# Shifting the start addresses of weights, operands and working buffers in SBUF by 32, 96 and 192 bytes

## What is computed

```
first block (1 layer):   x += g1 * ((gated sum of conv, HGRN2 and stick-breaking branches) @ w_out)
                         x += g2 * (square(relu(h2 @ mlp_w1)) @ mlp_w2)
second block (2 layers): x += 0.5 * swiglu(rms(x), ffn1_w_gate, ffn1_w_up, ffn1_w_down)
                         x += (sig(g_attn) * y_attn + sig(g_rnn) * y_rnn) @ w_out
                         x += 0.5 * swiglu(rms(x), ffn2_w_gate, ffn2_w_up, ffn2_w_down)
```

## Time and profile before

| | |
|---|---|
| median of three runs | 3328.55 us |
| profiled execution | 3327.95 us |
| its span, first to last instruction | 3326.2 us |
| granted TensorE clock | 0.999 |
| TensorE matmul busy | 3306.1 us, 17742 matmuls |
| weight loads busy | 2799.9 us |
| VectorE, ScalarE, GpSimd busy | 2169.9, 1466.6, 2127.7 us |

### The profile page before, as it was taken

The page is one execution under the profiler, slowest core; times in us unless marked ns, Lnnn a source line. Parts: engine busy times, 40 slices in busy tenths (PEclk is TensorE's granted clock), DMA queues, the critical chain, the costliest instruction groups (busy, mean ns, idle before and its releaser), DMA issues.

```text
span 3326.2 us, 52762 instructions
## 1 busy us (share of the span) xinstructions
PE 3306.1 (99%) x17742; PEld 2799.9 (84%) x17742; DVE 2169.9 (65%) x3377; ACT 1466.6 (44%) x2025; POOL 2127.7 (64%) x2188
## 2 busy tenths in 40 slices
PE   9999999999999999999999999999999999999999
PEld 5888777888889997788888899889987888888998
DVE  8887685544478878714435877788878334248886
ACT  4365664222243335735634333433347545533333
POOL 6444445555568886653356888698876544468886
PEclk9999999999999999999999999999999999999999
DMA  6221553322232323332223323232223222223232
GB/s 224 88 70 64 168 181 108 104 95 96 97 112 94 107 82 102 102 127 70 70 84 110 108 101 114 76 114 101 101 89 109 95 102 70 83 92 111 102 109 99
DMA packets 94485, 343.36 MB, mean 103 GB/s; under 512 B 10609, under 2 KB 11249, under 8 KB 93954
## 3 DMA queue, kind: packets, MB, share of 16 engines
q1 hardware_dynamic: 86978, 312.11, 27.4%
q10 hardware_dynamic: 7360, 29.29, 2.7%
HBM read 335.03 MB, written 2.13 MB: 101 GB/s over the span
## 4 chain that ended last, share of the span: by engine, by line
PE 52%; POOL 23%; issue 18%; DVE 2%; ACT 2%; DVEq 1%; POOLq 0%; ACTq 0%; DMA 0%
POOL w_lo L588 22%; PE ps L634 15%; PE ps L636 15%; PE ps L635 15%; POOL t_lo L588 1%; PE ps L1217 1%; PE ps L1199 1%; PE ps L801 1%; PE ps L802 1%; PE ps L803 1%; DVE arena L2771 1%; PE ps L1208 0%; DVEq L2773 0%; ACT w_hi L1305 0%; DVE arena L2172 0%
## 5 line engine op out<-in xcount | busy, mean ns | idle before, releaser
L588 POOL TENSOR_TENSOR w_lo<-raw,w_hi 128x256 fp32r<-128x256 f32 (+1 forms) x1680 | 1467.9, 904 | 1051.9 <-ACT w_hi L1305 1049.8
L634 PE MATMUL ps<-a_hi,w_lo 128*128 128x512 f32 (+1 forms) x2720 | 1019.3, 375 | 0.8 <-DVE a_lo L2118 0.3
L636 PE MATMUL ps<-a_hi,w_hi 128*128 128x512 f32 (+1 forms) x2720 | 1005.6, 370 | 0.0
L635 PE MATMUL ps<-a_lo,w_hi 128*128 128x512 f32 (+1 forms) x2720 | 1005.3, 370 | 0.0
L588 POOL TENSOR_TENSOR w_lo<-arena,w_hi 128x512 fp32r<-128x512 f32 x384 | 586.0, 1551 | 124.7 <-ACT w_hi L1785 121.3
L634 PEld LDWEIGHTS ps<-a_hi,w_lo 128*128 128x128 f32 x2720 | 512.6, 188 | 101.0 <-issue 18.3
L1305 ACT ACTIVATE w_hi<-raw 128x1024 fp32r<-128x1024 f32 x374 | 392.6, 1053 | 442.5 <-PE ps L636 424.0
L636 PEld LDWEIGHTS ps<-a_hi,w_hi 128*128 128x128 f32 x2720 | 512.6, 188 | 88.1
L635 PEld LDWEIGHTS ps<-a_lo,w_hi 128*128 128x128 f32 x2720 | 513.0, 189 | 81.2 <-issue 0.5
L634 PE MATMUL ps<-b_hi,w_lo 128*128 128x512 f32 x1088 | 425.9, 391 | 4.8 <-DVE b_lo L2190 4.0
L635 PE MATMUL ps<-b_lo,w_hi 128*128 128x512 f32 x1088 | 424.0, 390 | 0.0
(11 more groups left out here) (332 smaller groups left out, 4706.3 us busy)
## 6 DMA issues: line engine op xcount, KB each, us to landing
raw<-in_stream SPq DMA_DIRECT2D x471, 512.0 KB, 3.3
arena<-in_stream SPq DMA_DIRECT2D x96, 512.0 KB, 3.3
arena<-in_mod_w ACTq DMA_DIRECT2D x32, 512.0 KB, 4.2
arena<-in_mod_w SPq DMA_DIRECT2D x16, 512.0 KB, 11.6
arena<-arena ACTq DMA_DIRECT2D x16, 256.0 KB, 3.7
arena<-cum_rows ACTq DMA_DIRECT2D x2, 2048.0 KB, 9.2
xres<-in_x_t SPq DMA_DIRECT2D x4, 512.0 KB, 5.4
arena<-in_first SPq DMA_DIRECT2D x8, 256.0 KB, 11.8
```

The costliest lines, as they stand in the source:

```text
L588: last = pool.tensor_tensor(to[:, at], of[:, at], hi[:, at].bitcast(F32), ALU.subtract)
L634: pe.matmul(out, lo, x_hi, start=start, stop=False)
L635: pe.matmul(out, hi, x_lo, start=False, stop=False)
L636: return pe.matmul(out, hi, x_hi, start=False, stop=stop)
```

## The change

Three buffers that nothing reads or writes are put between the others, of 32, 64 and 96 bytes a partition:

```
         raw = sb("raw", [P, RING, D])
+        sb("shift_weights", [P, 8])
         w_hi = sb("w_hi", [P, RING, D], F32R)
         w_lo = sb("w_lo", [P, RING, D], F32R)
 
+        sb("shift_operands", [P, 16])
         a_hi, a_lo = sb("a_hi", [P, KT, S], F32R), sb("a_lo", [P, KT, S], F32R)
         b_hi, b_lo = sb("b_hi", [P, KT, S], F32R), sb("b_lo", [P, KT, S], F32R)
+        sb("shift_back", [P, 24])
         xres = sb("xres", [P, KT, S])
```

## The result

The changed kernel takes 3334.11 us (median of 20 runs, 3332.34 to 3334.91) against 3328.57 us (20 runs, 3327.69 to 3329.93): a ratio of 1.0016, interval 1.0009 to 1.0022. It is slower by 5.5 us, less than the 0.2% that the prediction counted as a change, and not the 28 us faster that it forecast.

What follows compares the result with a forecast made beforehand. The prediction took TensorE's matmul pitches as the bound: 28.2 us gained on a, b and streamed w, zero for all else, took 3327.95 to 3299.8 us, median 3300.3 us. The range was 3245 to 3375 us, the forecast's own 3283 to 3318.

Steps and rivals of the forecast that it cites:

- TensorE's pitches are the bound; no instruction moves; loads, rounding and subtraction take the same: Whole kernel: TensorE busy 3306.1 of 3326.2 us; issue cost nil, loads and ScalarE and GpSimd accesses costed at zero.
- What sets `t` and `q11` apart from `a` is where they start: 256-column matmuls: starts 32 bytes past a multiple of 64 give fixed parts of 11.3 and 10.0 ns, against 13.3.
- If the fixed part falls as it did there: 12,480 x 2.26 = 28.2 us: Matmuls on a, b and streamed w: each pitch's part beyond its columns shrinks 2.26 ns, gaining 28.2 us.
- The sign that the prediction named for 256 columns on `a`: Timeline after, 256 columns on a: pitch of some 117.7 ns where 120.0 stood.
- the one for 512 columns: Timeline after, undisturbed projection with 512 columns: pitch about 224.5 ns, against 226.8 before.
- `t` and `q11`: zero taken, between -4 and +6 us for `t`: Matmuls on t and q11, remainder by 64 now equal to the weights': zero; q11 between 0 and plus 2.5 us.
- At 1% other engines hold back little; GpSimd isn't the bound at 251 of 300 us: Fast chunks: GpSimd, busy 251.33 of 300 us, still isn't the bound with TensorE 1% quicker or itself 1% slower.
- No even step: Rival, 512-column stream: pitch stays at about 231.3 ns, 45 us slower, 3374 us; chance 0.22.
- Distance alone: Rival: only stream distance modulo 64 counts; t and q11 fall back to 120.0 ns, 8.7 us, 3337 us; chance 0.06.
- Nothing changes: Rival: a and b keep their distance from the weights modulo 64, t doesn't react; 3328.6 us; chance 0.17.

Runs made afterwards that it cites:

- common_shift32: Kernel before with weights, a, b, t, q11 and the working buffers all 32 bytes further, distances unchanged; 3328.83 us, ratio 1.0001.
- w32_only: Kernel before with only the rounded weights moved, to remainder 32 by 128; 3380.93 us, ratio 1.0157.
- back64_only: Kernel before with only t, q11 and the working buffers moved, to remainder 64 by 128; 3330.26 us, ratio 1.0005.

## Why the prediction was wrong

- *TensorE's pitches are the bound; no instruction moves; loads, rounding and subtraction take the same.* Right in the main. Loads into `raw` and the arena still land in 3.3 us, rounding takes 1061 ns as in the earlier trace rows (grouped view of the changed kernel below), GpSimd's subtraction of 512 columns takes 1361 ns from `raw` and 1562 from the arena in the mean, 1359 and 1551 before, and the pitches sum to the span's change. (These means differ by the buffer in either kernel; the two single rows, 1.30 and 1.31 us, didn't show it.)

```profile
L1788 ACT ACTIVATE w_hi<-arena 128x1024 fp32r<-128x1024 f32 x192 | 203.8, 1061 | 412.4 <-PE ps L639 412.4
```

- *What sets `t` and `q11` apart from `a` is where they start.* Wrong, and the root of the rest. In the earlier trace rows the moving start and its distance from the weights differ together; the prediction saw both and took the first. common_shift32 separates them: `a` at 32 with the weights at 32 keeps 120.0 ns with 256 columns and 226.7 with 512.

- *If the fixed part falls as it did there: 12,480 x 2.26 = 28.2 us.* **The step that failed**, carried from 256 to 512 columns because one pair of pitches (120.0 and 226.8) had the same fixed part. Measured: +17.2 us on the 9,984 with 512 columns; on the 960 short ones that stream `w` -5.0 us, more than twice the 2.2 us that the term gives them. On `a` itself, at the same new starts, the fixed part rose with 512 columns from 13.3 to 228.9 - 213.4 = 15.5 ns and fell with 256 to 117.8 - 106.7 = 11.1 ns. The sign that the prediction named for 256 columns on `a`, some 117.7 ns for 120.0, came; the one for 512 columns, 224.5 ns, came out the other way.

- *`t` and `q11`: zero taken, between -4 and +6 us for `t`.* The size was off and the bound too tight: without the waits `t` went from 364.3 to 353.4 us, 10.9 less. In the runs `t` stood anywhere from 113.3 to 120.2 ns, and the earlier trace rows showed one of these values.

- *At 1% other engines hold back little; GpSimd isn't the bound at 251 of 300 us.* Wrong where it mattered. The stretch view after still has GpSimd at 253.48 of 300 us:

```profile
2205.00:2505.00 300.00, 299.38 (x1965) 272.29 (x1964) 242.15 (x344) 114.65 (x137) 253.48 (x193) 1.00 0.28 97
```

But `t` got 4% faster, not 1%, and that mean hides the 15 us of each chunk in which GpSimd works without a gap (the rows above); 7.1 us more than before were waited at their end, (6.2 + 2.4) - (1.2 + 0.3). Part 4 of the page of the kernel before, the chain of work that ended last, had a sign of it that the prediction didn't use, GpSimd with 23%:

```profile
PE 52%; POOL 23%; issue 18%; DVE 2%; ACT 2%; DVEq 1%; POOLq 0%; ACTq 0%; DMA 0%
```

- *The rivals.* "No even step" had the mechanism, with 2.2 ns per long matmul instead of 4.5. It allowed the short ones 2,496 x 2.26 = 5.6 us; with `t` and `q11` they gave back 12.6, and the rest is 5.5 us, under the 0.2% counted as a change. w32_only shows what lay one shift away: 233.3 ns and 3381 us, above the range. "Distance alone" came nearest in time (3337 us for 3334.1), by luck: the distance was the better quantity, but by 64 it left 512 columns at 226.8 and took `t` up to 120.0, and neither came. "Nothing changes" (3328.6 us) is near by cancelling and not by its reason.

- The Trainium skill (TensorE: Matmul & The Clock Gate, Step-by-step: what each phase is for) says that loading the next tile's weights takes no SBUF read bandwidth from the running matmul. For float32r with a weight load per matmul the runs show that the weights' place isn't without effect on the running stream: moving the weights alone took its pitch from 226.7 to 233.3 ns. Whether read bandwidth is what is lost, no run shows.

No version beat both kernels: the nearest, common_shift32 and back64_only, can't be told from the kernel before.

## What to carry to other kernels

When the bound is a long run of matmuls with a weight load each, treat the start addresses of moving and stationary tiles as one setting: keep starts on multiples of 32 bytes, and measure the pitch at each distance, for each number of columns and for each choice of the moving side, since here the best distance for 512 columns (0) isn't where 256 columns reached their shortest pitch (64). Put every tile of a product in line, the low parts too, and don't add up parts measured alone. A stage that gets 4% faster needs its own look at who delivers to it, whatever the mean of the stretch says.

## What the runs showed of the hardware

- Several steady pitches, or three of them, are a multiple of about 6.67 ns: 226.7 = 34 x 6.67, 233.3 = 35 x 6.67, 120.0 = 18 x 6.67, 113.3 = 17 x 6.67; 3 x 228.9 = 686.7, 103 x 6.67 and 3 x 117.8 = 353.4, 53 x 6.67. 6.67 ns are 16 cycles at the granted 2.4 GHz. Others that the runs show, 118.7 and 117.3 ns, don't fit so, and why any do no run shows.
- At one pair of starts a stream can have two steady pitches (113.3 and 117.8 ns), and stretches of one execution fall into either.
- In every run with starts off multiples of 32 bytes the even step with 512 columns was gone: 231.1 and 235.5 ns (weights alone 8 and 16 off), 231.6 to 233.6 (weights, `a` and `b` 8, 16 or 24 off). The buffers were longer in these runs too, and the longer buffers alone were not tried.
